# Two-layer hybrid trunk: keys and queries split where they are made, maxima in row pairs, context work later, output gates two tiles ahead

## The reference

```python
h = rms_norm(x, prm['norm_g'][l]) * (1.0 + scale) + shift
u = h @ prm['w_in'][l]
...
s = jnp.einsum('bqgrd,bkgd->bgrqk', qblk, k).astype(jnp.float32) * scale
p = jax.nn.softmax(s, axis=-1).astype(v.dtype)
return jnp.einsum('bgrqk,bkgd->bqgrd', p, v)
...
out = jnp.concatenate([o_a, o_b, o_c, o_d], axis=-1) @ prm['w_out'][l]
x = x + gate * out
```

## Time and profile before

| what | value |
|---|---|
| device time, median of 3 runs | 4557.48 us (4557.45 to 4563.02) |
| the profiled execution | 4557.84 us, its span 4556.1 us |
| PE busy | 3877.5 us (85%) |
| DVE busy | 3036.5 us (67%) |
| ACT busy | 1430.7 us (31%) |
| POOL busy | 311.7 us (7%) |
| mean granted TensorE clock | 0.894 |
| attention, first layer | 1152.8 to 2045 us |
| heads, first layer | 592 to 870 us |
| output, first layer | 2045 to 2337.5 us |

### The profile page before, as it was taken

The page is one execution under the profiler, slowest core; times in us unless marked ns, Lnnn a source line. Parts: engine busy times, 40 slices in busy tenths (PEclk is TensorE's granted clock), DMA queues, the critical chain, the costliest instruction groups (busy, mean ns, idle before and its releaser), DMA issues. The chain is left out here.

```text
span 4556.1 us, 54296 instructions
## 1 busy us (share of the span) xinstructions
PE 3877.5 (85%) x18734; PEld 2767.3 (61%) x18734; DVE 3036.5 (67%) x5294; ACT 1430.7 (31%) x2566; POOL 311.7 (7%) x319
## 2 busy tenths in 40 slices
PE   5898979578599999987869897984868999999688
PEld 1897767355456555545759886773545656555366
DVE  1556957467477788856645397674756777888475
ACT  0651123211234444431136211331113444444311
POOL 0000000012100000001210000000220000000022
PEclk8899989767699999998989998995768999999799
DMA  7545445222201111114345353542220101110343
GB/s 289 192 142 154 148 139 143 73 77 60 52 18 27 32 29 29 32 35 170 134 141 187 123 179 119 143 124 73 66 61 22 25 24 38 40 30 11 110 141 117
DMA packets 338139, 427.17 MB, mean 94 GB/s; under 512 B 136808, under 2 KB 276456, under 8 KB 323328
## 3 DMA queue, kind: packets, MB, share of 16 engines
q1 hardware_dynamic: 328128, 353.01, 25.4%
q0 software_dynamic: 9792, 71.31, 5.0%
HBM read 279.84 MB, written 144.37 MB: 93 GB/s over the span
## 5 line engine op out<-in xcount | busy, mean ns | idle before, releaser
L2131 DVE TENSOR_REDUCE attn_mx<-attn_p 128x1 f32<-128x1024 f32 x512 | 625.4, 1222 | 299.1 <-PE attn_p L1923 298.2
L2110 ACT ACTIVATE attn_Pb<-attn_ST 128x1024 f32<-128x1024 f32 x544 | 549.8, 1026 | 860.9 <-PE attn_ST L1980 493.9
L2172 DVE TENSOR_TENSOR attn_acc<-attn_acc,attn_Pb 128x1024 f32<-128x1024 f32 x480 | 584.0, 1217 | 28.4 <-ACT attn_Pb L2110 26.4
L1992 PE MATMUL attn_OT<-attn_Pb,attn_V 128*64 128x512 f32 x2176 | 563.1, 633 | 0.0
L1923 PE MATMUL attn_p<-attn_K,attn_Q 96*128 96x512 f32 (+1 forms) x1024 | 370.7, 444 | 58.2 <-DVE attn_mx L2131 55.4
L1923 PEld LDWEIGHTS attn_p<-attn_K,attn_Q 96*128 96x128 f32 (+1 forms) x1024 | 172.7, 196 | 300.7 <-DVE attn_mx L2131 257.3
L522 PE MATMUL chan_b<-chan_hh,w_in_hi 128*128 128x256 f32 (+1 forms) x1152 | 328.7, 285 | 1.2 <-DVE w_in_lo L381 1.1
L523 PE MATMUL chan_b<-chan_hh,w_in_lo 128*128 128x256 f32 (+1 forms) x1152 | 325.8, 283 | 0.0
L524 PE MATMUL chan_b<-chan_hl,w_in_hi 128*128 128x256 f32 (+1 forms) x1152 | 325.8, 283 | 0.0
L841 DVE SCALAR_TENSOR_TENSOR gate_GY<-gate_win,gate_fw,gate_GY 128x1096 f32<-128x1096 f32 x240 | 311.7, 1370 | 0.4
L1992 PEld LDWEIGHTS attn_OT<-attn_Pb,attn_V 128*64 128x64 f32 x2176 | 132.3, 140 | 249.9 <-issue 207.6
(11 more groups left out here) (337 smaller groups left out, 7330.7 us busy)
## 6 DMA issues: line engine op xcount, KB each, us to landing
gate_ht<-scratch_HT POOLq DMA_DIRECT2D x34, 1024.0 KB, 6.2
head_ht<-scratch_HT POOLq DMA_DIRECT2D x34, 1024.0 KB, 5.8
mod_w<-in_w_mod SPq DMA_DIRECT2D x16, 1536.0 KB, 12.5
scratch_HT<-chan_hh SPq DMA_DIRECT2D x34, 512.0 KB, 3.3
scratch_HT<-chan_hl SPq DMA_DIRECT2D x34, 512.0 KB, 4.3
scratch_G<-gate_GT SPq DMA_DIRECT2D x34, 512.0 KB, 3.6
out_G<-scratch_G SPq DMA_DIRECT2D x34, 512.0 KB, 5.1
out_O<-scratch_O SPq DMA_DIRECT2D x34, 384.0 KB, 3.9
```

What stands on the lines that cost most here:

```text
L1992: mm = pe.matmul(OT[o * HD:(o + 1) * HD, :], V[par][:, kt, :], Pb[unit % NPB][:, o * 512:(o + 1) * 512], start=(kt == 0), stop=(kt == NKT ...
L2110: act.activation(Pb[unit % NPB][:, :], ST[unit % 2][:, :], ACT.Exp).then_inc(q["exp_done"], 1)
L2131: ins = dve.tensor_reduce(mx[:, t, w:w + 1], p1[:, :], AX.X, ALU.max)
L2172: ins = dve.tensor_tensor(sums[:, :], sums[:, :], prob[:, :], ALU.add)
```

## The change

Five parts, in the order of the program.

1. Scratch in DRAM: QT and KT become QM, KM (96-row heads) and QG, KG (64-row heads), each with high and low part. The modulation phase no longer stores 8 blocks of zeros into the unused rows. The heads phase and the cache phase store both parts; VectorE makes the low part from PSUM, in the heads phase as lows(n-2), after heads(n-1). The stores of tile n-2 wait for these. The transposes of tile n-2 move behind the small products of tile n-1.
2. Attention loads the split operands directly, from GpSimd's queue; hi and lo are gone, as are kraw and qraw. The context's operands come as 20 small loads and four GpSimd additions put high and low together again.
3. For 64-row heads the fill uses rows 0 to 63 for one half and rows 64 to 127 for the other; the low part of the keys no longer enters the maxima. The row of maxima is row 0 of Q2.
4. Block 0's fills alternate between p1 and ST[1]; the context's three pieces stand after fills 8, 12 and 15.
5. Output: gates(n+2) in body n; turn_conv(n+2) opens body n, turn(n+1) stands a quarter into it; gates(1) stands ahead of low(0); the residual is added by VectorE.

```diff
@@ modulation_phase, sync
-            for h in range(4, NH):
-                sp.dma_start(S.QT[h, HD:QK, :], zeros[:, 0:NT * P]).then_inc(stored, 16)
-                sp.dma_start(S.KT[h, HD:QK, :], zeros[:, :]).then_inc(stored, 16)
@@ heads_phase, sync
-                    sp.wait_ge(q["qst_ready"], m + 1 + START)
-                    sp.dma_start(S.QT[0:4, :, tok].rearrange("h r t -> r h t"), QST[:, :, :]).then_inc(q["q_stored"], 16)
...
+                    sp.wait_ge(q["qlow_ready"], m + 1 + START)
+                    sp.dma_start(S.QM[:, :, :, tok].rearrange("s h r t -> r (s h) t"),
+                                 QST[:, :, :, :].rearrange("r s h t -> r (s h) t").bitcast(F32)).then_inc(q["q_stored"], 16)
+                    sp.wait_ge(q["klow_ready"], m + 1 + START)
...
+                    sp.wait_ge(q["glow_ready"], m + 1 + START)
                     for o in range(2):
                         part = slice(o * HD, (o + 1) * HD)
...
+                        sp.dma_start(S.QG[o, :, :, :, tok].rearrange("k s r t -> r (k s) t"),
+                                     GST[part, 0:2, :, :].rearrange("r k s t -> r (k s) t").bitcast(F32)).then_inc(q["g_stored"], 16)
+                        sp.dma_start(S.KG[o, :, :, key].rearrange("s r t -> r s t"),
+                                     GST[part, 2, :, :].bitcast(F32)).then_inc(q["g_stored"], 16)
                 if 1 <= n <= NT:
                     sp.wait_ge(q["sq_ready"], n + START)
                     sp.dma_start(S.V[0:4, :, n, :].rearrange("h p d -> p h d"), KV[:, :, NOPE:P]).then_inc(q["v_stored"], 16)
@@ heads_phase, vector
+            def lows(m):
+                dve.wait_ge(q["qst_ready"], m + 1 + START)
+                dve.tensor_tensor(QST[:, 1, :, :], bQ[0:QK, :].rearrange("p (h t) -> p h t", h=4), QST[:, 0, :, :].bitcast(F32),
+                                  ALU.subtract).then_inc(q["qlow_ready"], 1)
...
-            for n in range(NT + 1):
-                means(n)
+            for n in range(NT + 2):
+                if n <= NT:
+                    means(n)
                 if n < NT:
                     latents(n)
-                if n:
+                if 1 <= n <= NT:
                     heads(n - 1)
+                if n >= 2:
+                    lows(n - 2)
@@ attention_phase, gpsimd
+            load(0)
+            zero(pool.memset(mtm[:, :, :], 0.0))
...
+            load(1)
+            pool.wait_ge(q["c_loaded"], 16 * 20 + START)
+            for t_ in (cQ, cK):
+                for rows, hs in ((slice(0, QK), slice(0, NMLA)), (slice(0, HD), slice(NMLA, NH))):
+                    summed(pool.tensor_tensor(t_[rows, 0, hs, :], t_[rows, 0, hs, :], t_[rows, 1, hs, :], ALU.add))
+            for h in range(2, NH):
+                pool.wait_ge(q["st_done"], (h - 1) * PER * NKT + START)
...
+                load(h)
@@ attention_phase, tensor
-                if B or r:
+                if B == 0:
+                    out = (p1, ST[1])[r % 2]
+                    if r >= 2:
+                        pe.wait_ge(q["red_done"], r - 1 + START)
+                else:
+                    out = p1
                     pe.wait_ge(q["red_done"], B * NKT + r + START)
...
+                        elif c == 0:
+                            qt, kt = Q1[par][0:HD, q0:q0 + P], K1[par][0:HD, k0:k0 + 512]
+                        else:
+                            qt, kt = Q2[par][HD:P, q0:q0 + P], K1[par][HD:P, k0:k0 + 512]
...
-                if r == 3:
+                if r == 8:
                     context_scores()
-                elif r == 8:
+                elif r == 12:
                     context_turn()
-                elif r == 12:
+                elif r == 15:
                     context_values()
@@ attention_phase, scalar and vector: hi() and lo() and their calls are removed
-                    if b == 0 and h + 1 < NH and 1 <= u <= len(hi_parts(h + 1)):
-                        hi(h + 1, u - 1)
...
-                    if b == 0 and u in (6, 9, 12, 15) and h + 1 < NH:
-                        lo(h + 1, u // 3 - 2)
@@ output_phase, tensor
+                if conv_next:
+                    turn_conv(n + 2, par, cnt + 1)
                 for half in range(2):
...
-                        if half and c == DC // 2 and turn_next:
+                        if half == 0 and c == DC // 2 and turn_next:
                             turn(n + 1, 1 - par)
@@ output_phase, vector
+            gates(1, 1, 0)
             low(0, 0)
...
-            def body(n, par, j, last):
-                if not last:
-                    gates(n + 1, 1 - par, j + par)
+            def body(n, par, j, more, ahead):
+                if ahead:
+                    gates(n + 2, par, j + 1)
+                if more:
                     low(n + 1, 1 - par)
...
+                dve.wait_ge(x_loaded[par], j * 16 + 16 + START)
+                emit(dve.tensor_tensor(Y[par][:, :], X[par][:, :], Y[par][:, :], ALU.add), y_ready, dve, n + 1)
@@ output_phase, gpsimd
-                pool.wait_ge(tch, n + 1 + START)
-                pool.wait_ge(x_loaded[par], j * 16 + 16 + START)
-                emit(pool.tensor_tensor(Y[par][:, :], X[par][:, :], Y[par][:, :], ALU.add), y_ready, pool, n + 1)
```

More of the change, by code:

```diff
@@ L1221, in _ @@
             act.wait_ge(kt_done, 1 + START)
[L1222 to L1223 removed]
+            step(act.activation(KST[:, 0, :, :], pk[0:QK, :], ACT.Copy))
+            emit(act.activation(GST[:, :, 0, :], pgk[0:HD, 0:2 * P].rearrange("p (o t) -> p o t", o=2), ACT.Copy), st_ready, act, 1)
         @block.vector
@@ L1910, in fill @@
                 h, b = divmod(B, PER)
-                par, rows = h % 2, (QK if is_mla(h) else P)
-                if B or r:
+                par = h % 2
+                if B == 0:
[4 more added lines that the diff above has]
+                    out = p1
                     pe.wait_ge(q["red_done"], B * NKT + r + START)
                 if r == 0:
-                    for t in range(NT_Q):
+                    for i in range(NT_Q):
+                        t = i // 2 + i % 2 * (NT_Q // 2)
                         q0 = b * QB + t * P
-                        mm = pe.matmul(p1[:, t * P:(t + 1) * P], Q1[par][0:rows, q0:q0 + P], K1[par][0:rows, LAT:KEYS], start=True, stop=True)
+                        if is_mla(h):
+                            qt, kt = Q1[par][0:QK, q0:q0 + P], K1[par][0:QK, LAT:KEYS]
+                        elif t < NT_Q // 2:
+                            qt, kt = Q1[par][0:HD, q0:q0 + P], K1[par][0:HD, LAT:KEYS]
+                        else:
+                            qt, kt = Q2[par][HD:P, q0:q0 + P], K1[par][HD:P, LAT:KEYS]
+                        mm = pe.matmul(out[:, t * P:(t + 1) * P], qt, kt, start=True, stop=True)
                 else:
@@ L2018, in _ @@
                 if b == PER - 1 and not last:
-                    pe.wait_ge(q["hi_ready"], HI0[h + 2] + START)
-                    pe.wait_ge(q["lo_ready"], LO0[h + 2] + START)
+                    for part in range(2):
+                        pe.wait_ge(K.qk_loaded[(h + 1) % 2][part], loads(h + 1, part))
                     if h + 1 in (NMLA, NMLA + 1):
@@ L2089, in output @@
                                    scale=rden[:, half * 4 + t:half * 4 + t + 1]).then_inc(q["o_ready"], 1)
-            for i in range(4):
-                hi(0, i)
             act.wait_ge(q["c_mx_ready"], 1 + START)
@@ L2370, in body @@
                 act.activation(oTh[par][:, :, :], pT[par][:, :], ACT.Copy).then_inc(ot_ready, 1)
-                if not last:
+                if more and not (isinstance(n, int) and n == 0):
                     square(n + 1, 1 - par, j + par)
@@ L2520, in __init__ @@
         self.ht_loaded = [x.enter_context(nc.semaphore(f"ht_loaded{i}")) for i in range(2)]
+        self.qk_loaded = [[x.enter_context(nc.semaphore(f"qk_loaded{i}{part}")) for part in "ab"] for i in range(2)]
 def build(nc, A):
```

288 lines of the change are left out of this document (141 added, 147 removed).

## The result

The changed kernel takes 4609.32 us in the median of 4 runs (4605.08 to 4610.16), the kernel before 4559.23 (4557.45 to 4563.02) on the same chip: a ratio of 1.0107, 95% interval 1.0089 to 1.0124. It is slower by 1.1%. The forecast was 4534 and its range ended at 4600. The profiled execution took 4609.76 us, with a span of 4608.0.

The account below looks back on a forecast made before the run. No one engine bounds the kernel; barriers separate phases. Heads +118, cache +3, modulation -3, attention -34 and -50, output -58 sum to -24: 4557.8 to 4534 us, range 4475 to 4600.

Parts of the forecast that it names:

- The ring: Heads: KV's copy, means, heads, subtractions, stores and KV's landing close in one turn of 18.4 us; +118 for both layers.
- the issues: Heads: SyncE's issues of four GST stores ahead of KV's store, put at 2.6 us.
- The landing of 2.6: Heads: time for KV's store to land after its issue starts, taken near the lower end of 1.9 to 5.5 us.
- Rival 1: Heads: KV's store lands late, after 5.5 us; the turn is 21.3, the whole 4621 us; chance 0.2.
- Rival 2: Heads: KV's store doesn't set the turn, TensorE does at 13.6 us; -24 instead of +118, whole 4392; chance 0.1.
- the wait at 2: Attention, after fill 8: TensorE waits 2 us for the context's operands, ready 18 to 30 us after the phase starts.
- the 17 us by which the first scores were to come earlier: Attention, before the first scores: earlier loads and two buffers save 17 us a layer, -34 for both.
- rival 4: Attention: the context's operands come 12 us or more after fill 8; 34 shrinks to 10, whole 4558; 0.2 with another rival.
- Splitting: Attention, 64-row heads: removing the splitting takes three blocks from 48.8 to 45.9 us, 8.7 a layer.
- The pairs: Attention, 64-row heads: fill halves in upper and lower rows overlap; about 2 us a block, 14 for seven blocks.
- the 2.3 forecast: Attention: gain from overlapping fill halves in the block before the seven 64-row blocks, 2.3 us a layer.
- the ring was put at 12.1: Output: square behind the high copy, then gates and low part, takes 12.1 us; body 12.5 with the loop's branch.

## Why the prediction was wrong, step by step

The sum was -24, measured was +51.9 in the profiled executions: 76 us. Of these, attention has 42, heads 19, the output 10, and the remaining terms 5. The largest single step that failed is the time at which the context's operands are ready.

**Heads, +137 for +118: mechanism right, size off by 19.** The ring closed where the prediction put it. From KV to the end of the subtractions it gave 13.1, and it is 13.07 (719.23 to 732.30). The terms that were short are the issues, 2.6 for four where they took 3.54 (732.34 to 735.88), one of them 1.45. The landing of 2.6 was 2.1 in most turns and 3.3 at the most. From the issue at 16.65 that makes 18.75 in most turns and up to 20, and not 18.4. Fifteen turns at 19.05 instead of 18.4 are 9.8 us, and a layer had 68.6 for 59; what the ends of the phase add and take nearly cancels. Rival 1, the late landing, didn't come here; it was measured when the store was moved half way forward, 4.2 us and more. The prediction named its cause, the doubled stores in front, and the two middle places of the store show it.

Rival 2 has its price: with the ring open the turn is 13.3, for 13.6 forecast, and the kernel 4434.6, where the rival said 4392 with the attention and output terms of the forecast. That is 43 us too low: in this kernel attention and output give 45 us each, 52 less than forecast in all, and heads give 11 more than it said.

**Attention, -42.5 for -84: four fifths of it one wait.** The context's operands were put at 18 to 30 us after the start and the wait at 2; in layer one the last of them landed at 36.5, and the wait was 17.78, in layer two 20.47. This step failed by 15.8 and 18.5 us, 34 in all. With it the 17 us by which the first scores were to come earlier were 1.5 in layer one, and in layer two they came 0.9 later. The first fill, forecast 3 us earlier, came 1.2 and 0.9 earlier. It was rival 4, with its condition (12 us or more after fill 8) met. The prediction had seen the pieces, 20 small loads and 6.4 MB beside them, and put their time without a row for it: the earlier trace rows has no two queues. What it left out was the delay of small loads by large ones, and issues of SyncE that stand for microseconds. The Trainium skill, "DMA: Bandwidth & Descriptors", says in its part on arbitration (section "Queues, rings and completion order") that an engine takes turns between queues, packet by packet. The trace is in line with it: 32 KB of keys took 16.1 us beside 6.49 MB of the other queue, and 11.1 with half of that beside them (queries 15.4 and 13.4). The prediction cited the rule and left it out of the sum.

The blocks of 64-row heads gave 23.6 a layer, for 22.7 forecast, but not by its steps. Splitting is 2.9 x 3 = 8.7, right. The pairs bring 1.2 a block at full clock (45.9 to 44.7), 8.2 for seven and not 14. A fill takes 0.43 instead of 0.56, 0.13 less, and the two neighbours of a pair of fills give 0.08 each back (two key tiles take 4.76 for 4.86). The Trainium skill, "TensorEngine Tiling (Array Packing)", Key Properties, says that a change of tiling mode drains the engine; the prediction worked 0.14 out of it, against 0.23 without, and measured is 0.13. VectorE is not the bound that the prediction made it: 38.90 us of work in 44.8, with TensorE busy for 44.35. The remaining 6.6 us are clock. Four of the seven blocks before had a spell at half clock, as this one (columns as above, kernel before), and none after:

```profile
1799.39:1846.90 47.51, 47.11 (x205) 26.55 (x205) 39.26 (x36) 19.94 (x27) 0.00 (x0) 0.96 0.22 47
```

So the right sum was luck: one term was too large and one wasn't there. The block before the seven brought nothing for the 2.3 forecast (1.1 us longer in one layer, 0.5 shorter in the other), and the blocks of 96-row heads lost 2.0 and 2.7 us a layer where the prediction had them unchanged, for the mixed rows.

**Output, -48.2 for -58.** The bound was named rightly, the square behind the high copy, but the ring was put at 12.1 and the body at 12.5, and it was 13.0 in the mean: 16 us over both layers. The gates(1) ahead of the first body took 7.5 us for 6.3, another 2.5. Against that the bodies of the kernel before, taken as 248.4 us from layer two, were 252.5 and 249.6, which gives 5 back; the remaining 3 are the prediction's rounding.

The term that failed is VectorE's gates, 5.04 from the earlier trace rows, taken from a tile in which GpSimd wasn't at work. The same steps now take 5.90 (4482.25 to 4488.15) in this tile, in which GpSimd's gates fall on VectorE's last ones:

```profile
4486.22 1.66 POOL L2474 TENSOR_TENSOR out_og<-out_G,out_O 128x256 f32<-128x256 f32 x2 [11.82 <-DMA out_G<-scratch_G]
...
4487.31 0.84 DVE L2435 TENSOR_TENSOR out_og<-out_G,out_c 128x256 f32<-128x256 f32 x1
```

VectorE's last two gates take 0.41 to 0.43 us in all 35 cases where GpSimd is idle, and 0.86 in the median of the 31 that fall mostly into its work. That GpSimd is the cause is argued from this coincidence; no run moved GpSimd's gates. The square's place, the other part of this ring, was tested.

**Cache and modulation.** The cache phases cost 2 us for 3. The stores of zeros, put at -3, brought nothing: heads start at 586.3 us, before at 586.2. Some 3 us more lie scattered in phases that the change doesn't touch.

**The chances.** Slower had 0.22, nearly all of it by rival 1. What came was rival 4 and smaller misses, nearly all on one side. A sum of +118 and -142 leaves a small number with the error of two large ones.

## What to carry to other kernels

Before a step is moved, write down for each queue what stands behind it, and give that its price before the gain is counted: here the place of one store of 128 KB, behind six others or ahead of them, was worth 175 us of 4609. The landing of a small transfer is not a constant: for this store it was 1.9 us with nothing in front and 4.2 behind 768 KB, and a load of 32 KB took 16 beside 6.5 MB of another queue. Where a small load gates an engine, issue the large ones that nobody waits for after it.

## What was not expected of the hardware

- **An issue can stand for microseconds.** SyncE's issue of a load of 32 KB takes 0.60 us, and 6.06, 4.20 and 3.41 us while 16 DMA engines are busy for 0.9 of the time. With 3.2 MB less beside them one of the sixteen stood for 6.59, the others for under 1 us. Why just these stand is open.
- **Half-clock spells go with the shape of the fills.** Of the seven blocks of a layer four had one with fills of 128 rows, none with pairs of 64, five and four with single halves of 64 rows. A spell at half clock lasts 3.4 us in most cases and then costs 1.6. What in the three kernels' work decides it was not tried.
- **Products of mixed height cost more than all of the larger height.** A block takes 53.8 us at full clock with 97, 96 and 96 rows, 53.4 with 97 throughout.
